# An encoder layer's recurrence: the triangular inverse by products over 128 partitions, with ScalarE laying out its operands

## The reference, cut to what matters

```python
def wkv7_scan(r, decay, k, v, kk_neg, kk_b, reverse):
    def step(state, inp):
        r_t, w_t, k_t, v_t, an_t, b_t = inp
        sa = jnp.einsum('bhij,bhj->bhi', state, an_t)
        state = (state * w_t[:, :, None, :] + sa[..., None] * b_t[:, :, None, :]
                 + v_t[..., None] * k_t[:, :, None, :])
        return state, jnp.einsum('bhij,bhj->bhi', state, r_t)
    ...
    _, ys = lax.scan(step, s0, xs, reverse=reverse)
```

## Time and profile before

| what | us |
|---|---|
| three timed runs | 5392.49, 5393.27, 5397.53; median 5393.27 |
| the profiled execution | 5393.33 |
| its span | 5391.5 |
| PE busy in the span | 4389.7 (81%), 61318 matmul records |
| DVE busy | 3113.5 (58%) |
| ACT busy | 2088.0 (39%) |
| POOL busy | 1069.9 (20%) |

### The profile page before, as it was taken

One profiled execution on the slowest core, in us unless ns is written; L12 is line 12 of the kernel. 1 busy time (PEld: TensorE's weight loads), 2 busy tenths in 40 slices (PEclk: granted clock), 3 DMA queues, 4 the chain that ended last, 5 costly groups with the idle time before them and its releaser, 6 DMA issues. The chain is left out here.

```text
span 5391.5 us, 144326 instructions
## 1 busy us (share of the span) xinstructions
PE 4389.7 (81%) x61318; PEld 3987.2 (74%) x61318; DVE 3113.5 (58%) x6054; ACT 2088.0 (39%) x4040; POOL 1069.9 (20%) x829
## 2 busy tenths in 40 slices
PE   5878888886688876777777768871399999999998
PEld 5756666664687875766767766651399999999998
DVE  6867777775688883444444445556644444444443
ACT  3347777774455551111111112220143343434433
POOL 4432222222133342110001212210101011010100
PEclk9989999999899998998999889995599999999999
DMA  7810000000433322122121124430255555555553
GB/s 159 157 46 13 16 13 14 15 12 24 154 122 134 132 102 97 52 62 60 53 62 56 57 70 142 152 112 0 67 161 170 164 163 166 162 168 167 166 162 105
DMA packets 496719, 526.60 MB, mean 98 GB/s; under 512 B 74224, under 2 KB 434672, under 8 KB 496240
## 3 DMA queue, kind: packets, MB, share of 16 engines
q1 hardware_dynamic: 390256, 413.95, 24.0%
q10 hardware_dynamic: 92480, 62.93, 5.0%
q0 software_dynamic: 13504, 42.30, 3.5%
HBM read 372.12 MB, written 146.99 MB: 96 GB/s over the span
## 5 line engine op out<-in xcount | busy, mean ns | idle before, releaser
L2339 DVE TENSOR_TENSOR g_wlo<-g_raw,g_whi 128x2048 fp32r<-128x2048 f32 x192 | 439.1, 2287 | 129.8 <-ACT g_whi L2301 129.8
L615 PE MATMUL sapS<-KT,saq 128*128 128x512 f32 x1024 | 369.2, 443 | 122.9 <-ACT saprob L515 115.0
L2301 ACT ACTIVATE g_whi<-g_raw 128x2048 fp32r<-128x2048 f32 x192 | 366.0, 1906 | 245.4 <-DMA g_raw<-expert_w_gate 245.4
L568 DVE TENSOR_REDUCE samx<-sapS 128x1 f32<-128x512 f32 x512 | 352.8, 689 | 184.4 <-PE sapS L615 179.1
L2406 PE MATMUL g_pD<-g_whi,g_hh 128*128 128x256 f32 (+1 forms) x1536 | 437.9, 285 | 0.6
L2406 PE MATMUL g_pD<-g_whi,g_hl 128*128 128x256 f32 (+1 forms) x1536 | 429.3, 279 | 0.0
L2406 PE MATMUL g_pD<-g_wlo,g_hh 128*128 128x256 f32 (+1 forms) x1536 | 429.0, 279 | 0.0
L523 ACT ACTIVATE saph<-sapT 128x512 fp32r<-128x512 f32 x512 | 305.7, 598 | 226.4 <-PE sapT L630 219.7
L505 POOL TENSOR_SCALAR saprob<-saprob,sarden 128x2048 f32<-128x2048 f32 x128 | 254.5, 1988 | 655.4 <-DVE sarden L587 655.4
L1116 PE MATMUL c_pP<-c_xh,c_whi 128*128 128x258 f32 x1120 | 335.4, 299 | 46.5 <-DMA c_gup<-g_lora_up 27.9
L515 ACT ACTIVATE saprob<-sapS,sanm 128x512 f32<-128x512 f32 x512 | 345.9, 686 | 9.7 <-DVE sanm L574 9.6
(11 more groups left out here) (386 smaller groups left out, 13887.0 us busy)
## 6 DMA issues: line engine op xcount, KB each, us to landing
g_raw<-expert_w_gate SPq DMA_DIRECT2D x64, 1024.0 KB, 5.0
g_raw<-expert_w_up SPq DMA_DIRECT2D x64, 1024.0 KB, 5.1
g_raw<-expert_w_down SPq DMA_DIRECT2D x64, 1024.0 KB, 5.0
ops<-c_ops SPq DMA_DIRECT2D x40, 1024.0 KB, 4.0
d_bd<-ops SPq DMA_DIRECT2D x80, 512.0 KB, 4.0
c_xh<-xT_hi SPq DMA_DIRECT2D x10, 1032.0 KB, 5.6
c_xl<-xT_lo SPq DMA_DIRECT2D x10, 1032.0 KB, 8.4
x_in<-x SPq DMA_DIRECT2D x20, 512.0 KB, 7.9
```

Of the source, the lines that this page charges most:

```text
L568: ins = dve.tensor_reduce(mx[:, h % 2, k:k + 1], pS[k][:], AX.X, ALU.max)
L615: mm = pe.matmul(pS[k][:], q[:, h // GH, h % GH, :], KT[:, 2 * (h // GH) + p, key0 + k * 512:key0 + (k + 1) * 512], start=(p == 0), stop=( ...
L2301: act.activation(w_hi[:, Q % NBUF, :, :], raw[:, Q % NRAW, :, :], ACT.Copy).then_inc(s["g_hi"], 1)
L2339: dve.tensor_tensor(w_lo[:, Q % NBUF, :, :], raw[:, Q % NRAW, :, :], w_hi[:, Q % NBUF, :, :].bitcast(F32), ALU.subtract).then_inc(s["g_lo" ...
```

## The change

Transposed copies of Z are no longer grown beside it. TensorE transposes Z of two tiles j at once (128x128, `turned_z`) before each level and once after the last, and ScalarE copies the result to `yq`, after the last level to `yf`. `x4` and `grown_y` are gone. The products of the inverse (`between`, `grown`), `through` and `solved` contract over all 128 partitions: one factor is laid out block-diagonally with zeros elsewhere (`zb`, `zsb`, `stb`, `tvb`, written by ScalarE in two copies of 64 partitions each; `pmq`, written by VectorE with a wider mask `pmask`), so one product serves both heads of a tile; its output is 64 partitions, the lower half for even j or the first head, the upper for the others. `zy` becomes `zc`, a single buffer.

The pairing of products is undone: each step stands by itself. In the turn the order is: transposes of the last Z, through, x1 and x3, solved, x2; then at each level transposes of Z, `between`, something else, `grown`. The something else is state at level 0, values at 1, turned at 2, out at 3, nothing at 4. ScalarE gets for each level two block copies and a copy of the transposes per direction. VectorE no longer updates Y, and does both states after level 0. Before the loop GpSimd makes an identity, and VectorE clears the new buffers and copies 40 pieces of masks.

```diff
+        br, kr, tbk, tvb, stb = [two(n, [P, RT, 2, C]) for n in "br kr tbk tvb stb".split()]
+        st, y_out = [two(n, [P, RT, C]) for n in "st yo".split()]
+        yf = two("yf", [P, RT // 2, 2, C])
+        one = lambda n, shape: [sb(f"d_{n}{g}", shape) for g in range(2)]
+        uu, tmp, zc = [one(n, [P, RT, C]) for n in "uu tmp zc".split()]
+        zb = one("zb", [P, RT, 2, C // 2])
+        yq = one("yq", [P, RT // 2, 2, C])
+        pmq = one("pmq", [P, RT // 2, 2, 2, C // 2])
+        zsb = one("zsb", [P, RT // 2, 2, 2, C])
+        pmask = sb("d_pmask", [P, 2, NL, 2, 2, C // 2])
+        eye = sb("d_eye", [P, P])
+        pX, pP, pT, pS = [[ps(f"d_p{n}{g}") for g in range(2)] for n in "XPTS"]
...
             def through(n, g):
                 act.wait_ge(s["d_zs"], 2 * n + g + 1)
-                act.activation(zs[g][:], slim(pS[g]), ACT.Copy).then_inc(s["d_zsc"], 1)
...
+            def blocks(m, l, g):
+                if l == 0:
+                    act.wait_ge(s["d_init"], 2 * m + g + 1)
+                else:
+                    act.wait_ge(s["d_Ze"], 2 * (NL * m + l - 1) + g + 1)
+                for h, rows in enumerate(halves):
+                    last = act.activation(packed4(zb[g][rows, :, h, :], l), cols4(zc[g][rows, :, :], l, g), ACT.Copy)
+                last.then_inc(s["d_zb"], 1)
+            def turned_z(m, par, l, g):
+                act.wait_ge(s["d_T"], 2 * ((NL + 1) * m + l) + g + 1)
+                y = yq[g] if l < NL else yf[par][g]
+                act.activation(y[:].rearrange("p a h t -> p (a h t)"), pT[g][:, 0:RT * C], ACT.Copy).then_inc(s["d_Te"], 1)
+            def state(n, par, g):
+                act.wait_ge(s["d_S"], 2 * n + g + 3)
+                for h, rows in enumerate(halves):
+                    last = act.activation(stb[1 - par][g][rows, :, h, :], st[1 - par][g][rows, :, :], ACT.Copy)
+                last.then_inc(s["d_Sb"], 1)
...
+            def level(m, l):
+                for g in range(2):
+                    blocks(m, l, g)
+                for g in range(2):
+                    turned_z(m, None, l, g)
             def turn(n, par, i, more):
+                m, other = n + 1, 1 - par
+                for g in range(2):
+                    turned_z(n, par, NL, g)
                 for g in range(2):
                     through(n, g)
                 for g in range(2):
                     solved(n, g)
-                    if more:
-                        keys(n + 1, 1 - par, g)
-                for g in range(2):
-                    if more:
-                        values(n + 1, 1 - par, g)
+                if not more:
+                    for g in range(2):
+                        out(n, par, i, g)
+                    return
+                for g in range(2):
+                    keys(m, other, g)
+                level(m, 0)
+                level(m, 1)
+                for g in range(2):
+                    state(n, par, g)
+                for g in range(2):
+                    values(m, other, g)
+                level(m, 2)
+                for g in range(2):
+                    turned(m, other, g)
+                level(m, 3)
                 for g in range(2):
                     out(n, par, i, g)
-                for g in range(2):
-                    if more:
-                        turned(n + 1, 1 - par, g)
...
+            for q, rows in enumerate(halves):
+                for g in range(2):
+                    for l in range(NL):
+                        for h in range(2):
+                            last = dve.tensor_copy(packed(pmask[rows, g, l, q, h, :], l), cols(beside[rows, g, l + 1, :], l, g))
+            last.then_inc(s["d_z"], 1)
+            dve.wait_ge(s["d_z"], 3)
...
+                flat = lambda t: t.rearrange("p a q h t -> p a q (h t)")
+                dve.tensor_tensor(flat(pmq[g][:]), bc(pP[g][:, 0:P].rearrange("p (a o t) -> p a o t", a=RT // 2, o=1), [P, RT // 2, 2, C]),
+                                  bc(flat(pmask[:, g, l:l + 1, :, :, :]), [P, RT // 2, 2, C]), ALU.mult).then_inc(s["d_Pe"], 1)
+            def grown(m, l, g):
+                    dve.wait_ge(s["d_Ze"], 2 * (NL * m + l - 1) + g + 1)
+                dve.wait_ge(s["d_Z"], 2 * (NL * m + l) + g + 1)
+                part = cols4(zc[g][:], l, g)
+                dve.tensor_tensor(part, part, packed4(grow(pP[g]), l), ALU.add).then_inc(s["d_Ze"], 1)
...
+                level(n + 1, 0)
+                for g in range(2):
+                    state(n, par, g)
+                for l in range(1, NL):
+                    level(n + 1, l)
...
+            def turned_z(m, l, g):
+                if l:
+                    pe.wait_ge(s["d_Ze"], 2 * (NL * m + l - 1) + g + 1)
+                else:
+                    pe.wait_ge(s["d_init"], 2 * m + g + 1)
+                    if m:
+                        pe.wait_ge(s["d_Te"], 2 * ((NL + 1) * (m - 1) + NL) + g + 1)
+                for a in range(RT // 2):
+                    mm = pe.transpose(pT[g][:, a * P:(a + 1) * P], zc[g][:, 2 * a:2 * a + 2, :].rearrange("p j t -> p (j t)"), eye[:])
+                mm.then_inc(s["d_T"], 1)
+            def between(m, par, l, g):
+                pe.wait_ge(s["d_zb"], 2 * (NL * m + l) + g + 1)
+                for j in range(RT):
+                    mm = pe.matmul(pP[g][halves[j % 2], j // 2 * C:(j // 2 + 1) * C], br[par][g][:, j, 0, :], zb[g][:, j, :, :].rearrange("p h t -> p (h t)"),
+                                   start=True, stop=True)
+                mm.then_inc(s["d_P"], 1)
+            def grown(m, l, g):
+                pe.wait_ge(s["d_Pe"], 2 * (NL * m + l) + g + 1)
+                pe.wait_ge(s["d_Te"], 2 * ((NL + 1) * m + l) + g + 1)
+                for a in range(RT // 2):
+                    for h, rows in enumerate(halves):
+                        mm = pe.matmul(pP[g][rows, RT * C + a * C:RT * C + (a + 1) * C], yq[g][:, a, h, :], pmq[g][:, a, :, h, :], start=True, stop=True)
+                mm.then_inc(s["d_Z"], 1)
+            def through(n, par, g):
+                if n:
+                    pe.wait_ge(s["d_Sb"], 2 * (n - 1) + g + 1)
+                for j in range(RT):
+                    flat = lambda m: m[:, j, :, :].rearrange("p h t -> p (h t)")
+                    to = pS[g][halves[j % 2], j // 2 * P:(j // 2 + 1) * P]
+                    pe.matmul(to, bd[par][g][:, j // 2, OP_A, j % 2, :], flat(stb[par][g]), start=True, stop=False)
+                    mm = pe.matmul(to, kr[par][g][:, j, 0, :], flat(tvb[par][g]), start=False, stop=True)
+                mm.then_inc(s["d_zs"], 1)
+            def solved(n, par, g):
+                pe.wait_ge(s["d_Te"], 2 * ((NL + 1) * n + NL) + g + 1)
+                for a in range(RT // 2):
+                    for h, rows in enumerate(halves):
+                        mm = pe.matmul(pS[g][rows, a * P:(a + 1) * P], yf[par][g][:, a, h, :], zsb[g][:, a, :, h, :], start=True, stop=True)
+                mm.then_inc(s["d_u"], 1)
...
+            def turn(n, more):
+                m, par = n + 1, (n + 1) % 2
+                for g in range(2):
+                    turned_z(n, NL, g)
+                for g in range(2):
+                    through(n, 1 - par, g)
+                if more:
+                    for g in range(2):
+                        x1(m, par, m // 2, g)
+                        x3(m, par, g)
+                for g in range(2):
+                    solved(n, 1 - par, g)
+                if more:
+                    for g in range(2):
+                        x2(m, par, g)
+                    for g in range(2):
+                        turned_z(m, 0, g)
+                    for g in range(2):
+                        between(m, par, 0, g)
+                for g in range(2):
+                    state(n, 1 - par, g)
+                if more:
+                    for g in range(2):
+                        grown(m, 0, g)
+                    for g in range(2):
+                        turned_z(m, 1, g)
+                    for g in range(2):
+                        between(m, par, 1, g)
+                    for g in range(2):
+                        values(m, par, g)
+                    for g in range(2):
+                        grown(m, 1, g)
+                    for g in range(2):
+                        turned_z(m, 2, g)
+                    for g in range(2):
+                        between(m, par, 2, g)
+                    for g in range(2):
+                        turned(m, par, g)
+                    for g in range(2):
+                        grown(m, 2, g)
+                    for g in range(2):
+                        turned_z(m, 3, g)
+                    for g in range(2):
+                        between(m, par, 3, g)
+                for g in range(2):
+                    out(n, 1 - par, g)
+                if more:
+                    for g in range(2):
+                        grown(m, 3, g)
+                    for g in range(2):
```

(66 more changed lines are left out.)

274 lines of the change are left out of this document (51 added, 223 removed).

## The result

| | us | runs |
|---|---|---|
| before | 5392.88 median (5380.17 to 5397.53) | 4 |
| after | 5594.43 median (5592.72 to 5596.74) | 4 |

The ratio is 1.0378, 95% interval 1.036 to 1.0396: slower by 202 us, where 28 were forecast. The span of the profiled execution is 5593.3 us. One of the ten executions of E11 took 5744.06 us, 6% more than the others, and is left out of its figures.

What follows compares the result with a forecast made beforehand. TensorE's instruction supply was taken to bound the recurrence. Steps summing to 28.65 us plus 0.75 for the clock gave 29.4 a turn, 0.6 more; 39 x 0.6 + 5 once = 28 us, so 5422, range 5310 to 5570.

Steps and rivals of the forecast that it cites:

- Supply: TensorE in the recurrence waits for its own instructions, one packet per 3.6 us at best; 6.2 us of stall a turn go.
- rival of serial halves: TensorE's products into alternating column halves do not overlap: +4.7, 34 us a turn, 5605 us; chance 0.12.
- Full drains: Each of eleven TensorE form switches costs 0.22 us: +1.4, 30.8 a turn, 5476 us; chance 0.16 together with slow copies.
- a switch: TensorE changing between forms with 64 and 128 rows: 0.1 us each, eleven a turn, 1.1 us.
- two in a row overlap: ScalarE's two block copies per level and direction: 0.28 us each, 0.17 apart, 0.45 for the pair, up to 0.56.
- step 5: Level 2 of the turn: four state and four value copies push ScalarE's blocks by 0.5 us; the level takes 4.4.
- Half of the low clock: The 3 us a turn at clock 0.50 behind the long stall are worth 1.5 us; 0.75 is kept.
- slow copies: Two ScalarE copies do not overlap, 16 x 0.11: up to +1.6 us a turn; chance 0.16 together with full drains.

Runs made afterwards that it cites:

- E11: Kernel before with the pairing of products undone, all products of one kind issued before all of the other: 5402.32 us, ratio 1.0025.
- E7: Kernel before without the loads of chunks 2 to 39, each chunk using what was loaded for the first two: 5337.12 us, ratio 0.9903.
- E3: Kernel after with the block layout made by VectorE, one masked product per direction and level, instead of ScalarE's block copies: 5402.55 us, ratio 1.0008.
- E1: Kernel after with ScalarE's four state copies moved from before level 2's blocks to behind level 4: 5494.46 us, ratio 1.0181.
- E10: Kernel after with the second of each pair of ScalarE's block, state and value copies left out, 14 a turn: 5381.9 us, ratio 0.9985.
- E6: Kernel after, blocks by VectorE, state and values over 64 rows, level 1's mask before the state update, through filling level 4: 5362.57 us, ratio 0.9956.
- E9: E6 with VectorE's state update moved behind level 2's mask, its four instructions interleaved over the directions: 5331.58 us, ratio 0.9897.
- E2: Kernel after with each ScalarE block copy over all 128 partitions, scaled by a 0/1 column, instead of over one half: 5566.06 us, ratio 1.0316.
- E4: Kernel after with state and values (through and solved) back to pair products over 64 rows, without the state's block copies: 5452.0 us, ratio 1.0101.
- E8: Kernel before with 64 more already satisfied semaphore waits a turn on TensorE, ahead of level 2's grown of direction 0: 5475.25 us, ratio 1.0162.

## Why the prediction was wrong

The direction was right, the size not: +0.6 us a turn were forecast and +4.95 measured.

**Right: what bounded the kernel before.** Supply was the limit (E7's rhythm, E11), and the change removed it: 153 packets in 1120 us are 4.6 a turn, as forecast, and the "issue" rows are 23 us, under the 60 named. TensorE's matmuls no longer wait for VectorE's masks (18.7 us before in the window of 1120 us, no row after); the forecast had named those of level 1. Of the loads the forecast made too much: without them the kernel before gains 1.3 us a turn, and the stalls stay (E7).

**Right: the array.** Products over 128 partitions into alternating column halves overlap. 16 records of `grown` take 0.69 to 0.72 us, (0.69 - 0.22)/15 = 0.031 apart, where 0.029 or 0.055 stood open. `through` ran even at the pair's pace, 1.8 us for 2.6 taken. That hid another error: x1, x3 and x2 took 0.5 us more than their terms, since records of 128 columns were 0.055 us apart ((1.09 - 0.27)/15 for x1) and not 0.050. The rival of serial halves, whose price of 5605 is near the measured time, is refuted by these rows and by E3: the same products fit into a turn of 28.9 us. Full drains did not come at their price either: `values` issues its last record at 2604.48 + 1.15 - 0.22 = 2605.41, and grown, in the other form, starts 0.15 us later, 0.12 more than the pace, where a switch was taken at 0.1 and a full drain priced at 0.22. Behind records of 128 columns (0.27 us long) the next form starts after 0.20, 0.15 more than the pace. Over eleven switches that is 0.2 to 0.6 us a turn more than forecast, not 1.4.

**Wrong: the price of ScalarE's copies.** The step is "two in a row overlap, as VectorE's do ..., so I take 0.17 apart, 0.45 for the pair". It took VectorE's overlap for that of ScalarE's half-partition pairs, which have none. Measured are 4 block copies in 1.28 us, (1.28 - 0.31)/3 = 0.32 apart: P of direction 1 starts 2.22 us after grown for 1.64, and what is placed there 2.6 for 1.95. That is 0.6 us in each of levels 3 and 4 and in level 0; the other 0.5 us of the end lies between level 4's grown and `through` (1.75 us for 1.25), which waits for the later direction. VectorE lays out both directions' blocks in 0.76 us for 1.28 (E3).

**Wrong: step 5, ScalarE comes late in level 2 by 0.5 us.** Eight copies at 0.17 apart were in the sum; they take 1.71 + 1.56 us and push the blocks by 1.6. The order of work had been read rightly, and its price came from the same wrong spacing. So level 2 took 7.71 us for 4.4: 1.1 us more of lateness, 0.6 for the spacing of the block copies themselves, and the 1.5 us of the slow clock below.

**Wrong: the clock.** Half of the low clock (0.75 us) was kept as a round sum, from one stretch of 3 us a turn in the earlier trace rows. The clock of 0.90 in the earlier trace rows says more: (1 - 0.90) x 28.8 / 0.5 = 5.8 us a turn at half. In the kernel after, the idle 1.6 us of level 2 does what the stall of 3 us did in the earlier trace rows: 3.5 us at 0.53, 1.5 us a turn. It is not a cost of its own: E1 removed the wait and it went, the clock from 0.95 to 1.00.

The forecast did have a case "slow copies", up to +1.6 us a turn. It priced only the missing overlap, 16 x 0.11 (which is 1.8, not 1.6), and left out what a late copy sets off behind it. The missing overlap itself measured 0.15 us a block copy (0.32 - 0.17), 0.22 a value copy and 0.26 a state copy. By E10 leaving out half of the copies is worth 33.75 - 28.5 = 5.25 us a turn, wait and clock with it.

## What to carry to other kernels

Before an engine is given a new row of small instructions, take their spacing from rows of that engine and that shape; a duration is no spacing, and the overlap of another engine, or of another shape on the same one, does not carry over. In-order queues turn such a spacing into a wait where copies that nobody needs yet stand ahead of the one on the chain: move those first (E1 took 100 us off with no instruction removed), then look where the moved work is late next (E6, E9). And where TensorE stalls every 128 records for "issue", pairing its products for a faster pace buys next to nothing (13 us of 5389 in E11); what removed the stalls was fewer instructions.

## What the runs showed that was not expected

- Two of ScalarE's half-partition block copies cost what two over all 128 partitions cost: 64x128 four in 1.28 us, 128x128 with a scale four in 1.28 us (E2). Copies of 64x256 were 1.56 (from PSUM) and 1.71 us for four, yet two of 128x256 in one piece from PSUM take 0.66 us, so that the second starts 0.28 behind the first. The four over 64 partitions alternate between the halves and do not overlap; those over 128 do (E2), and so do copies over the first half alone (E10). Why stays open.
- Level 2's idle time on TensorE, 1.59 us in the kernel after and 1.38 in E2, was followed by a stretch at half clock (about 3.5 us) in most turns: 29 such stretches in the 32 turns from 2060 to 3140 us of the kernel after, 23 in E2, two in E1, where that wait is 0.33 us. Waits of 0.8 us in E4 and of 1.18 in E6 left the clock at 1.00 over the window.
- A wait on a semaphore long since reached cost TensorE 34 ns each in E8, with whatever the 64 of them did to the supply and the clock.
- Without pairing the array is no faster than the supply: the records of `state` in E11 are 4 per 0.117 us, 128 in 3.7 us, which is the rhythm of the packets.
